# RWKV-7 products with b and kd side by side as one stationary, and contractions over stacked [b; k] and [u; v]

## The reference

```python
def rwkv7_step(S, inp):
    r, w, k, v, kk, b = inp
    sa = jnp.einsum('bhvk,bhk->bhv', S, -kk)
    S = S * w[:, :, None, :] + sa[..., None] * b[:, :, None, :] + v[..., None] * k[:, :, None, :]
    y = jnp.einsum('bhvk,bhk->bhv', S, r)
    return S, y
...
    kk = l2norm(heads(k * k_k), 1e-12)
    k = k * (1.0 + (a - 1.0) * k_a)
...
    S, y = lax.scan(rwkv7_step, wkv0.astype(f32),
                    (tmaj(r_h), tmaj(w_h), tmaj(k_h), tmaj(v_h), tmaj(kk), tmaj(kk * a_h)))
```

## Time and profile before

| | |
|---|---|
| median of 3 runs | 1988.0 us (1987.83 to 1988.33) |
| the profiled execution's own time | 1992.14 us |
| its span | 1990.3 us |
| mean granted clock of TensorE | 0.966 |
| TensorE busy | 1863.0 us (94%) |
| VectorE busy | 1253.5 us (63%) |
| ScalarE busy | 937.7 us (47%) |
| POOL busy | 76.7 us (4%) |

### The profile page before, as it was taken

The page is one execution under the profiler, slowest core; times in us unless marked ns, Lnnn a source line. Parts: engine busy times, 40 slices in busy tenths (PEclk is TensorE's granted clock), DMA queues, the critical chain, the costliest instruction groups (busy, mean ns, idle before and its releaser), DMA issues.

```text
span 1990.3 us, 45265 instructions
## 1 busy us (share of the span) xinstructions
PE 1863.0 (94%) x19300; PEld 1691.2 (85%) x19300; DVE 1253.5 (63%) x2189; ACT 937.7 (47%) x1840; POOL 76.7 (4%) x155
## 2 busy tenths in 40 slices
PE   5999989989999988989999999899899998789998
PEld 3899978878888777788989999788799888679997
DVE  3555356677456776778556654577754586769863
ACT  3334455454456534433444444654454764353343
POOL 0000000121000200000000000001200011000000
PEclk8999999999999989999999999999999998889999
DMA  8877756556565566699765666554553546359873
GB/s 261 241 216 225 210 164 183 156 154 162 146 175 150 153 171 158 185 282 269 216 197 155 181 176 182 166 147 136 149 139 104 149 123 159 93 145 273 242 199 110
DMA packets 556519, 353.37 MB, mean 178 GB/s; under 512 B 19620, under 2 KB 515270, under 8 KB 555022
## 3 DMA queue, kind: packets, MB, share of 16 engines
q1 hardware_dynamic: 490634, 302.74, 53.7%
q10 hardware_dynamic: 60756, 38.81, 7.4%
q0 software_dynamic: 4928, 8.92, 1.8%
HBM read 332.27 MB, written 18.50 MB: 176 GB/s over the span
## 4 chain that ended last, share of the span: by engine, by line
PE 76%; DVE 10%; DMA 6%; ACT 4%; issue 3%; POOL 1%; ACTq 0%; SPq 0%; DVEq 0%; POOLq 0%
PE bank L903 73%; DMA ring<-in_ffn_up 3%; DMA ring<-in_w_ada 3%; PE bank L652 2%; DVE ring_r L725 2%; DVE far L1984 1%; ACT w_hi_r L717 1%; DVE big L1984 1%; DVE y L1984 1%; DVE big L609 1%; POOL far L628 1%; DVE big L608 1%; DMA far<-t_blocks 1%; DVE big L1987 1%; DVE h L1987 0%
## 5 line engine op out<-in xcount | busy, mean ns | idle before, releaser
L903 PE MATMUL bank<-big_r,w_hi_r 128*128 128x264 f32 x4160 | 1075.2, 293 | 49.6 <-DVE h_r L1987 24.3
L903 PE MATMUL bank<-big_r,ring_r 128*128 128x264 f32 (+1 forms) x3456 | 991.0, 287 | 0.0
L903 PEld LDWEIGHTS bank<-big_r,w_hi_r 128*128 128x128 f32 x4160 | 744.8, 190 | 111.6 <-issue 90.0
L903 PE MATMUL bank<-h_r,w_hi_r 128*128 128x264 f32 x2752 | 793.8, 288 | 0.1
L725 DVE TENSOR_TENSOR ring_r<-ring,w_hi_r 128x1024 fp32r<-128x1024 f32 (+2 forms) x440 | 523.6, 1195 | 382.3 <-ACT w_hi_r L717 378.6
L717 ACT CAST w_hi_r<-ring 128x1024 fp32r<-128x1024 f32 (+2 forms) x440 | 451.9, 1028 | 454.0 <-PE bank L903 195.1
L903 PEld LDWEIGHTS bank<-big_r,ring_r 128*128 128x128 f32 (+1 forms) x3456 | 659.3, 191 | 1.3 <-issue 0.3
L903 PEld LDWEIGHTS bank<-h_r,w_hi_r 128*128 128x128 f32 x2752 | 527.1, 192 | 1.6 <-issue 0.5
L903 PE MATMUL bank<-ring,c 128*32 128x256 f32 x1152 | 93.8, 405 | 15.1 <-DMA ring<-in_w_ada 12.7
L903 PE MATMUL bank<-big,far 64*64 64x64 f32 (+2 forms) x1440 | 104.9, 257 | 0.0
L903 PEld LDWEIGHTS bank<-big,far 64*64 64x64 f32 (+1 forms) x1440 | 88.2, 141 | 11.4 <-issue 10.9
(11 more groups left out here) (300 smaller groups left out, 1838.1 us busy)
## 6 DMA issues: line engine op xcount, KB each, us to landing
ring<-in_ffn_up SPq DMA_DIRECT2D x176, 512.0 KB, 4.8
ring<-in_w_in SPq DMA_DIRECT2D x148, 512.0 KB, 3.8
ring<-in_w_ada SPq DMA_DIRECT2D x144, 512.0 KB, 4.5
ring<-in_ffn_down SPq DMA_DIRECT2D x64, 512.0 KB, 4.5
far<-in_state_gdn_ssm ACTq DMA_DIRECT2D x28, 512.0 KB, 6.2
ring<-in_ffn_down SPq DMA_DIRECT2D x32, 384.0 KB, 3.5
ring<-in_w_out SPq DMA_DIRECT2D x16, 512.0 KB, 4.9
out_sample_gdn_ssm<-far ACTq DMA_DIRECT2D x16, 512.0 KB, 5.1
```

The source lines that it names most:

```text
L903: return pe.matmul(out, lhsT, rhs, start=start, stop=stop)
```

## The change

b and kd of a head pair are stored side by side in one buffer of three columns of 64 a chunk (`bkd`: kd, b, kd), so that the first head reads [b, kd] and the second [kd, b] as one stationary of 64 rows and 128 columns. One matmul then gives both products of a head, b's on one half of the partitions and kd's on the other, and another gives both transposes. v is transposed to the other half than the one that it comes from (`HALVES[1 - hd]`), so that for each head the tokens of b and u lie on one half and those of k and v on the other. `stacked` and `tok` replace `prod_b`, `prod_k`, `btok`, `ktok`. The state update and the inner part of the output contract over all 128 partitions, [b; k] with [u; v]; for that POOL copies v next to u (`us_v`, `values(c)`), and TensorE waits for these copies before step 2. The product of the k triangle with v in step 0 reads one half of the partitions and writes the other; for chunks 1 to 3 it is issued after all products with the old state, and TensorE waits for its own semaphore `ws_done` between the two. The output's products with the old state are likewise issued first, all together. VectorE has three operations where it had two for b and kd. ScalarE's negation and the writes of the inverse for runs 0 and 1 are split by halves.

```diff
-        prod_b = part(big, WORK, 2 * UNITS, 2 * C)
-        prod_k = part(big, WORK + 4096, 2 * UNITS, 2 * C)
-        ktok = part(big, WORK + 8192, 2 * UNITS, C)
-        btok = part(big, ZG + 2112, 2 * UNITS, C)
+        stacked = [part(big, WORK + 4096 * hd, 2 * UNITS, 2 * C) for hd in range(2)]
+        tok = [part(big, at, 2 * UNITS, C) for at in (ZG + 2112, WORK + 8192)]
+        us_v = part(big, ZG + 1088, 2, NT, C)
...
+            for rows, tri in triangles(run):
+                act.copy(tri[rows, :, 0:B16], both[rows, :, 0:B16, 1])
+                i = act.copy(tri[rows, :, B16:48], both[rows, :, B16:48, 0])
+            i.then_inc(inv_c.sem, inv_c.one())
...
+                for rows, tri in triangles(run):
+                    i = dve.tensor_tensor(tri[rows, :, 48:C], columns(both, 1, 48)[rows], whole_bank(3, B16)[rows], ALU.add)
...
+                    def values(c):
...
+                            pool.wait_ge(y_done.sem, y_done.at(c))
...
+                        for hd in range(2):
+                            at = HALVES[1 - hd]
+                            i = pool.tensor_copy(us_v[at, hd, :, :], pa[at, 2 * NT:3 * NT, c * C:(c + 1) * C])
+                        i.then_inc(pool_done.sem, pool_done.one())
...
-                            for bank, by in ((4, b_f), (5, kd_f)):
-                                for hf in HALVES:
-                                    mm(banks[bank][hf, 2 * t0:2 * t1].rearrange("p (a t) -> p a t", a=2), by[hf, t0:t1],
-                                       pa[hf, j:j + NT + 1:NT, t0:t1])
-                            for bank, at, of in ((3, 0, pa[:, 2 * NT + j, :]), (3, 256, kd_f), (2, 0, b_f)):
-                                for hf in HALVES:
-                                    i = mm(banks[bank][hf, at + t0:at + t1], of[hf, t0:t1], ident64[hf, :])
+                            both_of = [bkd[hf, c, (1 - hd) * C:(3 - hd) * C] for hd, hf in enumerate(HALVES)]
+                            for hd, hf in enumerate(HALVES):
+                                mm(banks[4 + hd][:, 2 * t0:2 * t1].rearrange("p (a t) -> p a t", a=2), both_of[hd],
+                                   pa[hf, j:j + NT + 1:NT, t0:t1])
+                            for hd, hf in enumerate(HALVES):
+                                mm(banks[3][HALVES[1 - hd], t0:t1], pa[hf, 2 * NT + j, t0:t1], ident64[hf, :])
+                            for hd, hf in enumerate(HALVES):
+                                i = mm(banks[2 + hd][:, 256 * hd + t0:256 * hd + t1], both_of[hd], ident64[hf, :])
...
+                            for j in range(NT if c else 0):
+                                for hf in HALVES:
+                                    i = mm(banks[2][hf, j * C:(j + 1) * C], pa[hf, NT + j, t0:t1], m_old[hf, j, :], j == 0, False)
+                            if c:
+                                i.then_inc(ws_done.sem, ws_done.one())
+                                pe.wait_ge(ws_done.sem, ws_done.at(2 * c))
                             for j in range(NT):
-                                u = j * NC + c
-                                for hf in HALVES:
-                                    out = banks[2][hf, j * C:(j + 1) * C]
-                                    if c:
-                                        mm(out, pa[hf, NT + j, t0:t1], m_old[hf, j, :], True, False)
-                                    i = mm(out, prod_k[hf, u, C:2 * C], pa[hf, 2 * NT + j, t0:t1], c == 0, True)
+                                for hd, hf in enumerate(HALVES):
+                                    v_at = HALVES[1 - hd]
+                                    i = mm(banks[2][hf, j * C:(j + 1) * C], stacked[hd][v_at, j * NC + c, C:2 * C],
+                                           pa[v_at, 2 * NT + j, t0:t1], c == 0, c == 0 or j == NT - 1)
...
+                            pe.wait_ge(pool_done.sem, pool_done.nth(POOL_SETUP + NC * l + c + 1))
                             for j in range(NT):
-                                    mm(out, btok[hf, u, :], us_a[hf, j, :], True, False)
-                                    i = mm(out, ktok[hf, u, :], pa[hf, 2 * NT + j, t0:t1], False, True)
+                                for hd, hf in enumerate(HALVES):
+                                    i = mm(banks[4][hf, j * C:(j + 1) * C], tok[hd][:, j * NC + c, :], us_v[:, hd, j, :])
...
+                            for j in range(NT if c else 0):
+                                for hf in HALVES:
+                                    mm(banks[5][hf, j * C:(j + 1) * C], m_old[hf, j, :], pa[hf, j, t0:t1], j == 0, False)
                             for j in range(NT):
-                                    mm(out, us_a[hf, j, :], prod_b[hf, u, 0:C], c == 0, False)
-                                    i = mm(out, pa[hf, 2 * NT + j, t0:t1], prod_k[hf, u, 0:C], False, True)
+                                for hd, hf in enumerate(HALVES):
+                                    i = mm(banks[5][hf, j * C:(j + 1) * C], us_v[:, hd, j, :], stacked[hd][:, j * NC + c, 0:C],
+                                           c == 0, c == 0 or j == NT - 1)
...
-                            tt(b_f, kb_t, e_n)
-                            tt(kd_f, kp_t, e_n)
+                            tt(bkd[:, :, C:2 * C], kb_c, e_c)
+                            for hd, hf in enumerate(HALVES):
+                                tt(bkd[hf, :, 2 * (1 - hd) * C:(3 - 2 * hd) * C], kp_c[hf], e_c[hf])
```

More of the change, by code:

```diff
@@ L64 @@
 Y_BANKS = (4, 1)
+POOL_SETUP = 3
 B16 = 16
@@ L318, in build @@
         solve_bufs += [[pa[:, NT, 0:NPR], part(big, (NT + 1) * T, B16, B16, 2), pa[:, NT + 3, 0:NPR]]]
-        inv_sets = [(g_lt if n == 2 else prod_b[:, UNITS * n:UNITS * (n + 1), C:2 * C], part(big, inv_t_at[n], UNITS, C, 2),
+        inv_sets = [([g_lt] * 2 if n == 2 else [x[:, UNITS * n:UNITS * (n + 1), C:2 * C] for x in stacked], part(big, inv_t_at[n], UNITS, C, 2),
                      part(big, inv_x_at[n], UNITS, C)) for n in range(3)]
@@ L572, in gather @@
             for rows, cols, part_of in blocks():
-                pool.dma_start(lt_blocks[part_of, :, :].rearrange("u s t -> s u t"), lt[rows, :, cols]).then_inc(block_in.sem, block_in.one())
+                pool.dma_start(lt_blocks[part_of, :, :].rearrange("u s t -> s u t"), lt[rows.start // C][rows, :, cols]).then_inc(block_in.sem, block_in.one())
         def fetch(pool, run):
@@ L651, in invert, with triangles @@
                         out, moving = banks[s][hf, u * n:(u + 1) * n], columns(both[hf], 0, C - n, u)
-                    i = pe.matmul(out, x_b[hf, u, :] if s else lt[hf, u, :], moving, start=True, stop=True)
+                    i = pe.matmul(out, x_b[hf, u, :] if s else lt[hd][hf, u, :], moving, start=True, stop=True)
             i.then_inc(inv_pe.sem, inv_pe.one())
+        def triangles(run):
+            lt = inv_sets[run][0]
+            return [(slice(0, P), g_lt)] if run == 2 else [(hf, lt[hd]) for hd, hf in enumerate(HALVES)]
         def settled(act, run):
@@ L666, in invert_dve @@
             if s == 3:
-                dve.tensor_tensor(lt[:, :, 48:C], columns(both, 1, 48), whole_bank(3, B16), ALU.add).then_inc(inv_t.sem, inv_t.one())
+                for rows, tri in triangles(run):
+                    i = dve.tensor_tensor(tri[rows, :, 48:C], columns(both, 1, 48)[rows], whole_bank(3, B16)[rows], ALU.add)
+                i.then_inc(inv_t.sem, inv_t.one())
                 dve.wait_ge(inv_t.sem, inv_t.all())
@@ L2165, in prep @@
                             us = slice(j * NC, (j + 1) * NC)
-                            for dst, bank in ((prod_b, 4), (prod_k, 5)):
-                                i = tt(dst[:, us, :], banks[bank][:, :].rearrange("p (u t) -> p u t", u=NC),
+                            for hd in range(2):
+                                i = tt(stacked[hd][:, us, :], banks[4 + hd][:, :].rearrange("p (u t) -> p u t", u=NC),
                                        bm(masks[:, :, :].rearrange("p a t -> p (a t)"), NC))
```

41 lines of the change are left out of this document (22 added, 19 removed).

## The result

The changed kernel takes **2000.1 us** in the median of 4 runs (1997.09 to 2003.75), the kernel before 1987.9 (4 runs). The estimated ratio is 1.0054 with an interval of 1.0031 to 1.0077. Two more series of 6 runs each gave 1.0077 [1.0052, 1.0101] and 1.0055 [1.0035, 1.0075]. So the change makes the kernel about 0.6% slower, where I had forecast no measurable difference and a range that ended at 1994.

What follows compares the result with a forecast made beforehand. TensorE, busy for 94% of the span, was taken as the bound. Terms 5.2 - 13.5 + 1.6 + 3.8 + 0.35 = -2.55 us, from the median 1988.0, gave 1985.4 us, range 1979 to 1994.

Steps and rivals of the forecast that it cites:

- 16 calls of products: Products stage on TensorE: each call 0.32 us slower through changes of tile form, +5.2 us over 16 calls.
- VectorE's operation, before `ones_half`: Products: the third VectorE operation, 0.335 us, delays TensorE before most of 16 bonus products, +3.8 us, bounds 0 and 5.4.
- recurrence, with the self-wait: Recurrence on TensorE: 64 fewer records a chunk give -13.5 us over both layers; TensorE's wait for itself gives back +1.6.
- the self-wait: Step 0 of chunks 1 to 3: TensorE waits for itself before the cross products, 0.26 us, six times +1.6 us.
- inverse: Triangular inverse, run 0 of layer 0: its last step becomes two VectorE operations, delaying ScalarE's clearing, +0.35 us (0 to 0.7).
- The group becomes 0.564 + 0.29 = 0.854: Products, one chunk's group: 0.564 us of passes plus 0.29 for two changes of form, 0.068 us slower than before.
- the opening: Start of a products call: 128 moving columns in the new form take another 0.05 us.
- The drain itself: Products, each change of tile form: the next matmul starts 0.07 us before the last one's modelled end, costing 0.097 us.
- POOL's copies: Recurrence: POOL's eight copies of v a layer cost nothing, covered by 12.7 us for chunk 0 and 13.4 for chunk 1.
- rivals A: Products: no drain between the 64-row forms, so a call is 0.84 us faster, total 1966.8 us; chance 0.07.
- rival C: Products and step 0: crossed tiles' halves run one after the other, 14.8 us more, total 2000.2 us; chance 0.09.
- B, the hidden operation: Products: VectorE's third operation is hidden behind other work, total 1981.6 us; chance 0.20.

Runs made afterwards that it cites:

- four changes a group: Changed kernel with the two v matmuls of a group placed apart, around the wide product pair: 2045.52 us, ratio 1.0275 to the kernel before.
- third operation, 64 partitions: Kernel before with kd made in two VectorE operations of 64 partitions: 1998.95 us, ratio 1.0053.
- third operation, full width: Kernel before with one more VectorE operation of 128 partitions, its result unused: 1991.39 us against 1984.85, ratio 1.0032.
- one change a call: Changed kernel with each products call reordered, all v first, then products, then transposes: 1977.82 us, ratio 0.9944 to the kernel before.
- one change a call, again: The same reordered kernel run once more, beside the changed kernel on one chip: 1980.48 us against 2001.39.
- split products: Changed kernel with each wide product and transpose matmul split into two of 64 columns: 1974.64 us, ratio 0.9926 to the kernel before.
- split, two VectorE operations: The split products kernel with VectorE's two full-width operations for b and kd put back: 1962.02 us, ratio 0.9889 to the kernel before.
- with the new recurrence: The kernel of split, two VectorE operations, with the next chunk's crossed k and v products moved into step 1: 1950.31 us, ratio 0.9834.

## Why the prediction was wrong

Each term of the sum against what the traces show. Terms of the changed kernel at the full clock:

| term | predicted | shown |
|---|---|---|
| 16 calls of products | +5.2 | +7.7 (16 x 0.48) |
| VectorE's operation, before `ones_half` | +3.8 | +3.6 |
| recurrence, with the self-wait | -11.9 | -13.4 |
| inverse | +0.35 | +1.4 |
| sum | -2.55 | -0.7 |
| TensorE at the lower clock | no term | 14 to 26 us more at it in the touched stages, worth 6 to 11 |

1. **The failed step is the sum itself, which has no term for the clock**: "The sum: 5.2 - 13.5 + 1.6 + 3.8 + 0.35" holds passes and waits at the full clock alone. The terms came within 2 us of their sum. What a us at the lower level costs can be read from a group of a call: 1.56 us there and 0.91 at the full clock, so 0.65 of 1.56, or 0.42 of the time at that level. The next table takes only the stages that the change touches, in each trace against that of the kernel before: the products with the inverses and the recurrences, before from 276.56 to 669.23 us and from 1228.12 to 1635.15. The terms are those of the same trace: 16 times the call's difference to 3.29, the idle time before `ones_half`, the recurrence (-13.4, with the new one -20.9) and the inverse's two waits in layer 0.

| trace | terms | more at the lower level | 0.42 of it | sum | these stages | whole kernel (means) |
|---|---|---|---|---|---|---|
| changed | -0.7 | 13.7 | +5.7 | +5.0 | +5.5 | +12.6 |
| changed, second series | -0.2 | 26.0 | +10.9 | +10.7 | +10.5 | +15.5 |
| changed, third series | +0.1 | 13.7 | +5.7 | +5.8 | +8.5 | +10.9 |
| four changes a group | +17.3 | 92.2 | +38.7 | +56.0 | +54.0 | +54.8 |
| third operation, 64 partitions | +4.9 | 13.4 | +5.6 | +10.5 | +10.3 | +9.8 |
| third operation, full width | +2.7 | 2.4 | +1.0 | +3.7 | +2.1 | +6.2 |
| one change a call | -19.1 | 23.9 | +10.0 | -9.1 | -9.6 | -10.3 |
| one change a call, again | -19.3 | 26.2 | +11.0 | -8.3 | -8.6 | -9.8 |
| split products | -24.8 | 0.0 | 0 | -24.8 | -23.2 | -14.6 |
| split, two VectorE operations | -30.7 | 3.4 | +1.4 | -29.3 | -29.7 | -21.9 |
| with the new recurrence | -38.8 | 3.0 | +1.3 | -37.5 | -37.3 | -32.7 |

In these stages the terms and the clock together come within 3 us of every trace. So in the changed kernel's three traces the missing term is 6 to 11 us, and the sized terms were 2 to 3 us too low. The stages that the change doesn't touch differ from trace to trace by -9 to +6 us. The one trace of the kernel before took 1992.1 us, 4 more than its median, so a mean can lie some 4 us above what the touched stages give. For the changed kernel it lies 2 to 7 above, for the last three rows 5 to 9; where the rest of that lies is open.

Why the clock falls is open as well. Sixteen changes of form a call bring it down: in that run seven calls with no idle time right before them ran partly at the lower level. At eight it isn't shown. The six such calls in the three traces of the changed kernel all stand behind an idle piece of 1.7 to 2.7 us, and the kernel with one change a call has no less time at the lower level in these stages (24 and 26 us more than before, against 14, 26 and 14). Idle pieces alone don't do it either: the split products have pieces as long (1.69 and 2.71 us) and all their calls run at the full clock. What the alternation at eight changes costs for certain is the passes and drains: 16 x 1.23 = 19.7 us between 3.77 and 2.54 us a call.

2. **"The group becomes 0.564 + 0.29 = 0.854"** was too small: 0.91. The first pass after a change of form is longer by 0.05, and I counted it so. But the product pair follows the transposing pair within one form, and its first pass is longer as well (0.165 against 0.112 for a next one of that form). The earlier trace rows show exactly this in the row at 723.87, 128 columns moving after 64. I had counted it once a call as "the opening" and not in each group. 3 x 0.05 is the missing 0.16 a call, 2.6 us. The drain itself was right, in place and size, and so the Trainium skill's rule (TensorEngine Tiling (Array Packing), Key Properties) agrees with the trace.

3. **VectorE.** The sum was right and its parts were not. I priced the added operation like one of 128 partitions (0.335); by the two changes of halves that it brings it costs 0.52 to 0.53. That alone would have given +5.2, as the run with kd in two operations shows. In the changed kernel most pieces grew by the same 0.53, but the last one shrank from 2.18 to 1.36 us, since the call ahead of it ran at the lower clock for 6.04 us and covered it. So 3.8 came out by accident: the idle time was hidden by a call that was longer still. The two other traces of the changed kernel have +4.6 and +4.5.

4. **The inverse.** That VectorE's operation "is what ScalarE's clearing at 463.56 waits for" held before and no longer holds. I put ScalarE's two more copies at nothing, with 3 us of room. They stand ahead of the clearing in its own queue: +0.64 us, and the DMAs behind it took another 0.9 longer. With 0.1 us less in the wait of the inverse before it, that is the +1.4 (+1.0 and +1.4 in the two other traces). No room of 3 us stood ahead of the clearing.

5. **Right:** recurrence (step 2 at 2.02 as predicted, 3.24 for 3.4), the self-wait (0.24 for 0.26), no new wait there, POOL's copies hidden, rivals A and C out. B, the hidden operation, is out by the idle time. The measured 2000.1 us is the number of rival C (2000.2), but by chance, since its mechanism isn't there. The gain lies in stretches at the full clock, where a us counts once, and the loss in those where the clock falls.

6. **The range** was built from the bounds of terms that the trace had. Its worst case was +0.7 us, and the clock's spread in the kernel before alone (0.963 to 0.975, 1976 to 1998 us over 48 runs) was wider than the range's upper half; its medians in the four series lie between 1984.9 and 1989.7.

## What to carry to other kernels

Before tiles are made wider, look whether crossed tiles are free: here four 64x64 tiles side by side gave in 1.97 us what wide tiles gave in 3.77, without a change of form. If two forms are needed, group them, so that the form changes once and not in each group. And look at the clock of each stretch before adding up: here 5.2 us of idle time added ahead of the small matmuls cost about 10, with 13 us more at the lower level, while time saved in the recurrences, at the full clock, counted once. A mean clock of the whole execution doesn't show this; compare the same stage in both traces. Last, when an operation is split by halves of the partitions, count the changes of half and not the elements.

## What the runs showed of the hardware

- Four tiles of 64x64 start 0.007 us apart and run side by side, crossed ones included. I had known it only for pairs; the Trainium skill counts four (TensorEngine Tiling (Array Packing), Available Configurations, and not Key Properties, which says that different tiles can run their matmuls in parallel), and the split run now shows it.
- VectorE operations of 256 elements that start on the same half of the partitions as the one ahead follow after 0.335 to 0.345 us, and one that starts on the other half only after the full 0.42. So one operation made into two by halves took 0.53 us more, and an extra one of full width 0.34. Four operations of 64 partitions on one half overlap (0.19 to 0.21 apart, 0.27 to 0.30 long).
- With 16 changes of form in each call TensorE's mean granted clock was 0.948, with 8 it was 0.960 to 0.964 in three series, with one or none 0.964 to 0.969. Only the step to 16 is clear of the spread.
- A stretch at the clock's lower level cost 0.42 of its length: a group of a call took 1.56 us there and 0.91 at the full clock.
